# The first mixer's VectorE order: the decay matrix ahead of the convolution taps in slots 2 to 5

## The chip, the cores and the metric

The program runs on one core of a Trainium2 chip. The metric is the device time of one execution in microseconds, lower is better.

## The reference

Two model blocks one after the other, on 512 rows of width 1024, in float32. The change lies in the first mixer of the first block, a state space mixer with 32 heads in 8 groups and chunks of 128 rows, run in both directions:

```python
def step(state, inp):                       # one chunk of 128 rows
    cum = jnp.cumsum(lac, axis=1)
    decay = jnp.exp(jnp.where(causal, cum[:, :, None] - cum[:, None], -jnp.inf))
    xdt = xc * dtc[..., None]
    cb = jnp.einsum('blgn,bsgn->blsg', cc, bc)
    y = jnp.einsum('blsgr,bsgrp->blgrp', cb[..., None] * decay, xdt)
    y = y + jnp.einsum('blgn,bgrpn->blgrp', cc, state) * jnp.exp(cum)[..., None]
    ...                                     # new state
def ssd_mixer(u, w_in, conv_w, ...):
    z, xbc, dt = jnp.split(u @ w_in, ...)
    xbc = jax.nn.silu(dwconv(xbc, conv_w, conv_b))      # five taps
    y = ssd_scan(forward) + rev(ssd_scan(reversed)) + xh * d_skip
    y = rmsnorm(y * jax.nn.silu(z)) @ w_out             # per group
```

After it come a second mixer (gated linear attention), a convolution and attention block, cross attention and an MLP; the change does not touch them.

## The kernel before

All large products are *streamed*. A unit of weights (128 x 1024 numbers, 0.5 MB) is loaded by SP into `weights_raw`, rounded by ScalarE into `weights_hi` (`split_hi`, line 137), and the rest of the rounding is made by VectorE into `weights_lo` (`split_lo`, line 147), which also frees `weights_raw` for a load. TensorE then makes three matmuls for each tile of weights (`mm3`, lines 79 to 81), 24 for a unit, into one of three PSUM banks named `stream` (SB = 3). Tile t uses bank t % 3, and `stream_products` waits for `bank_free` of the tile three before it:

```python
        if t >= SB:
            pe.wait_ge(c.bank_free[t % SB], t // SB)
```

The mixer (`ssd_stage`, line 315) runs in rounds i = 0 to 9 of eight slots k = 0 to 7. In round i, g = i - 1 is the group whose chunks are computed, f = i - 2 the group whose output is normed and multiplied out. Slots 0 and 1 stream the gate z, slots 2, 3, 5 and 6 the four convolution inputs (`CONV`: two tiles of `ssd_x`, then two of `ssd_bc`) of group i, slots 4 and 7 (`SSD_OUT`, from round 2 on) an output unit: four tiles of six matmuls each, every one into its own bank. Rounds 2 to 7 are full; round 1 has nothing in slots 4 and 7; round 8 has no convolution inputs.

Each engine has its own program of the slots, written out by hand, and executes it in order; the loop `for i, k in slots` in each part sets that order. In slot k:

- TensorE streams the slot's unit; then in slots 2 to 4 it makes the state contributions (line 752), in slots 2 to 5 `y_intra(g, k - 2)` (line 734), which multiplies `ssd_m` of block k - 2, and in slots 1 to 4 `decay_sums(g, k - 1)` (lines 708 to 711), the sums from which the decay of block k - 1 is computed.
- ScalarE starts the convolution of the tile of the slot before (centre tap and bias, line 856), rounds the weights of the unit two ahead, and in slots 2 to 5 takes the exponential of the decay sums (`ssd_work`, line 919; semaphore `s_decay`).
- POOL makes in slots 2 to 5 the backward part of block k - 2 (line 681) and in slots 1 to 4 the four step tensors `ssd_la_steps` for the decay sums (line 693), which wait for the decay sums before.
- VectorE adds the other four taps to the convolution of the tile of the slot before (line 983; the last of them frees the bank), closes the output tiles of the slot before (`close`, line 952: adds bank to `h` and frees it), makes the weight rest of the unit two ahead, closes the first output tile of this slot, and then comes to the three operations of the decay matrix for block t = k - 2 (lines 1057, 1061, 1066): `ssd_cb` times dt, plus the backward part, times the decay. The third waits for `s_decay` of its block. After them come the state operations (lines 1074 to 1082) and, in slot 2, the norm of group f (lines 1088, 1091).

Of the kernel before, what the change touches and what calls it, by code (L numbers as in the profile page):

```python
# [15 lines left out]
ALU = mybir.AluOpType  # L16
AX = mybir.AxisListType

P = 128
# [10 lines left out]
HPG = SH // SG  # L30
# [53 lines left out]
def spread(ap, n):  # L84

    return ap.rearrange("p (a o) -> p a o", o=1).broadcast_to([ap.shape[0], ap.shape[1], n])


def again(ap, n):

    return ap.rearrange("p (o a) -> p o a", o=1).broadcast_to([ap.shape[0], n, ap.shape[1]])
# [223 lines left out]
def ssd_stage(nc, c, A, plan, gain):  # L315
# [8 lines left out]
    with ExitStack() as ctx:  # L324
# [4 lines left out]
        dtc = sb("dt_cols", [P, NT, 64])  # L329
# [249 lines left out]
        decay, t1, t2 = (work[:, j, :] for j in range(3))  # L579
        xw = mb("xw", [P, 2, 3, GW])  # L580
        bt = mb("b_tok", [P, T])
        cbm = mb("cb", [P, 2, T])
        rhs = mb("la_steps", [P, 4, HPG, P], F32R)
        mm = mb("m", [P, 2, HPG, P])
# [18 lines left out]
        G = range(SG)  # L603
        CONV = {2: 0, 3: 1, 5: 2, 6: 3}

        def conv_tile(g, j):
            return (2 * g, 2 * g + 1, 2 * SG + g, 3 * SG + g)[j]
# [11 lines left out]
        def head(cols, d, t, g):  # L619
            return cols[:, t, 32 * d + HPG * g:32 * d + HPG * (g + 1)]  # L620
# [4 lines left out]
        def before(i, k):  # L625
            return (i, k - 1) if k else (i - 1, NU - 1)

        def tile_of(i, k):
            return c.tiles_before[plan[i, k]]
# [310 lines left out]
        def _(dve):  # L940
# [30 lines left out]

            for i, k in slots:
                g, f = i - 1, i - 2
                pi, pk = before(i, k)
                if (pi, pk) in plan and pk in CONV:
                    cj = CONV[pk]
                    t, ct = tile_of(pi, pk), conv_tile(pi, cj)
# [48 lines left out]
                if k == 1 and g in G:  # L1026
# [13 lines left out]
                    for d, t0, nt in ((0, 0, 2), (0, 2, 1), (1, 1, 1), (1, 2, 2)):  # L1040
# [5 lines left out]
                                src[:, u * GW:(u + 1) * GW].rearrange("p (h m) -> p h m", h=HPG),  # L1046
                                spread(w[:, u, :], HD), ALU.mult)
                        ins.then_inc(s_xw, 1)
                if 2 <= k <= 5 and g in G:
                    t = k - 2  # L1050
                    m = 3 * (4 * g + t)
                    v = t1.rearrange("p (h l) -> p h l", h=HPG)
                    if t == 0:
                        dve.wait_ge(s_cbm, 2 * g + 2)
                    if 4 * g + t:
                        dve.wait_ge(s_m, m)
                    dve.tensor_tensor(v, again(cbm[:, 0, t * P:(t + 1) * P], HPG),  # L1057
                                      spread(head(dtc, 0, t, g), P), ALU.mult).then_inc(s_m, 1)
                    dve.wait_ge(s_m, m + 1)
                    dve.wait_ge(s_t2, 4 * g + t + 1)  # L1060
                    dve.tensor_tensor(t1, t1, t2, ALU.add).then_inc(s_m, 1)  # L1061
                    dve.wait_ge(s_m, m + 2)
                    dve.wait_ge(s_decay, 4 * g + t + 1)
                    if 4 * g + t >= 2:
                        dve.wait_ge(s_y, 4 * g + t - 1)
                    dve.tensor_tensor(mm[:, t % 2, :, :].rearrange("p h l -> p (h l)"), t1, decay, ALU.mult)\  # L1066
                       .then_inc(s_m, 1)
                if 3 <= k <= 5 and g in G:
                    j = k - 3
                    dve.wait_ge(s_con, 3 * g + j + 1)  # L1070
# [2008 lines left out]
```

## Time and profile before

| | us |
|---|---|
| median of three timed runs | 1860.97 (1857.37 to 1861.91) |
| the profiled execution | 1857.3, span 1855.6 |
| TensorE busy | 1735.0 (94%) |
| VectorE busy | 1189.9 (64%) |
| ScalarE busy | 769.0 (41%) |
| POOL busy | 408.1 (22%) |

Times are counted from the span's start. The first mixer's rounds 1 to 8 lie between some 62 and 580 us. A matmul row shows when the matmul began and its modelled duration; consecutive ones overlap, so the distance of their starts is their price. In square brackets stands how long the engine sat idle before a row, and whom it waited for.

### The profile page before, as it was taken

The page shows a single profiled execution, that of the slowest core. Times are in us where ns is not written, and L with a number is a line of the kernel's source. Part 1 is how long each engine was busy: PE and PEld are TensorE (multiplying, and loading weights), DVE is VectorE, ACT ScalarE, POOL GpSimd, SP SyncE. Part 2 cuts the span into 40 slices and gives each one's busy share as a digit, 9 for nine tenths or more (in the row PEclk, how much of TensorE's full clock was granted, in tenths as well). Part 3 has the DMA queues.
Part 4 walks back from the last instruction along what each step waited for, and adds up shares of the span by engine and source line. Part 5 has one row for each costly group of instructions (what it writes and reads, how often), then busy time and mean ns, then how long its engine had stood idle before and what let it go on. Part 6 is the DMA issues. An engine that isn't in the chain of part 4 may idle for free.

```text
span 1855.6 us, 21247 instructions
## 1 busy us (share of the span) xinstructions
PE 1735.0 (94%) x8104; PEld 1404.2 (76%) x8104; DVE 1189.9 (64%) x1587; ACT 769.0 (41%) x1143; POOL 408.1 (22%) x351
## 2 busy tenths in 40 slices
PE   6989999999987999999999889999999999999997
PEld 4767777787765777878777677888778778888886
DVE  6868878877966747575757676777665553434343
ACT  5333444343343435444445344446454442324232
POOL 0444644653563100000002501222120110000001
PEclk9989999999988999999999899999999999999999
DMA  3312222222210322222212223222323233333331
GB/s 102 91 35 68 67 70 57 60 66 69 57 49 25 86 54 65 80 79 69 76 54 87 63 74 80 62 59 80 103 82 103 88 91 91 103 91 102 92 101 69
DMA packets 253772, 139.18 MB, mean 75 GB/s; under 512 B 26013, under 2 KB 248134, under 8 KB 253670
## 3 DMA queue, kind: packets, MB, share of 16 engines
q1 hardware_dynamic: 253670, 137.82, 26.1%
q8 instruction: 65, 1.06, 0.2%
q14 instruction: 37, 0.30, 0.1%
HBM read 135.70 MB, written 2.10 MB: 74 GB/s over the span
## 4 chain that ended last, share of the span: by engine, by line
PE 58%; DVE 22%; ACT 9%; issue 7%; POOL 4%; DMA 1%; ACTq 0%; DVEq 0%; SPq 0%; POOLq 0%
PE stream L79 16%; PE stream L81 16%; PE stream L80 16%; DVE weights_lo L147 3%; ACT weights_hi L137 2%; DVE ssd_x L983 2%; DVE ssd_work L1061 1%; DVE ssd_bc L983 1%; DVE ssd_work L1057 1%; DVE ssd_y L1088 1%; PE q L1978 1%; PE q L2002 1%; POOL ssd_y L653 1%; PE q L79 1%; PE q L81 1%
## 5 line engine op out<-in xcount | busy, mean ns | idle before, releaser
L79 PE MATMUL stream<-u_lo,weights_hi 128*128 128x512 f32 (+2 forms) x1312 | 525.3, 400 | 17.0 <-DVE h L952 5.1
L81 PE MATMUL stream<-u_hi,weights_hi 128*128 128x512 f32 (+2 forms) x1312 | 514.7, 392 | 0.0
L80 PE MATMUL stream<-u_hi,weights_lo 128*128 128x512 f32 (+2 forms) x1312 | 514.6, 392 | 0.0
L147 DVE TENSOR_TENSOR weights_lo<-weights_raw,weights_hi 128x1024 fp32r<-128x1024 f32 (+4 forms) x269 | 336.3, 1252 | 270.2 <-ACT weights_hi L137 269.9
L137 ACT ACTIVATE weights_hi<-weights_raw 128x1024 fp32r<-128x1024 f32 (+4 forms) x269 | 268.5, 1000 | 444.9 <-PE stream L81 430.4
L79 PEld LDWEIGHTS stream<-u_lo,weights_hi 128*128 128x128 f32 (+2 forms) x1312 | 247.7, 189 | 81.0 <-issue 12.4
L81 PEld LDWEIGHTS stream<-u_hi,weights_hi 128*128 128x128 f32 (+2 forms) x1312 | 247.3, 188 | 54.2 <-issue 0.4
L80 PEld LDWEIGHTS stream<-u_hi,weights_lo 128*128 128x128 f32 (+2 forms) x1312 | 247.4, 189 | 53.9 <-issue 2.9
L217 POOL COPY h_sum_of_squares<-h_squares 128x512 f32<-128x512 f32 x5 | 3.2, 648 | 796.9 <-ACT h_squares L205 796.9
L79 PE MATMUL stream<-mlp_a_lo,weights_hi 128*128 128x512 f32 x256 | 100.2, 391 | 0.0
L81 PE MATMUL stream<-mlp_a_hi,weights_hi 128*128 128x512 f32 x256 | 99.7, 389 | 0.0
L80 PE MATMUL stream<-mlp_a_hi,weights_lo 128*128 128x512 f32 x256 | 99.6, 389 | 0.0
L653 POOL TENSOR_TENSOR ssd_y<-ssd_y,ssd_state_parts 128x384 f32<-128x384 f32 x32 | 33.0, 1032 | 184.3 <-DVE ssd_state_parts L969 182.0
L2853 DVE SCALAR_TENSOR_TENSOR mlp_relu<-stream,h_squares 128x512 f32<-128x512 f32 x32 | 22.1, 691 | 70.2 <-PE stream L81 70.1
L1947 POOL TENSOR_TENSOR mix_conv<-mix_conv,att_tap_products 128x512 f32<-128x512 f32 x30 | 40.2, 1341 | 121.6 <-ACT att_tap_products L2061 119.6
L983 DVE SCALAR_TENSOR_TENSOR ssd_bc<-stream,params,ssd_bc 128x510 f32<-128x510 f32 (+1 forms) x64 | 48.0, 749 | 28.6 <-ACT ssd_bc L856 26.9
L220 POOL TENSOR_TENSOR h_sum_of_squares<-h_sum_of_squares,h_squares 128x512 f32<-128x512 f32 x34 | 48.6, 1428 | 71.3 <-ACT h_squares L205 69.7
L79 PE MATMUL stream<-ssd_y_lo,weights_hi 128*128 128x512 f32 x128 | 53.2, 416 | 8.5 <-DVE ssd_y_lo L1091 5.2
L734 PE MATMUL q<-ssd_m,ssd_x_pair 128*128 128x128 f32 x256 | 36.8, 288 | 22.8 <-DVE ssd_m L1066 22.8
L2130 DVE SCALAR_TENSOR_TENSOR q<-mix_z,params,q 128x512 f32<-128x512 f32 x76 | 57.1, 751 | 1.7
L734 PEld LDWEIGHTS q<-ssd_m,ssd_x_pair 128*128 128x128 f32 x256 | 33.0, 196 | 31.0 <-DVE ssd_m L1066 30.1
L693 POOL TENSOR_TENSOR ssd_la_steps<-mask_ge,ssd_la_hi_cols 128x512 fp32r<-128x512 f32 x32 | 39.3, 1229 | 75.1 <-DVE ssd_la_lo_cols L1009 41.5
(484 smaller groups left out, 3155.9 us busy)
## 6 DMA issues: line engine op xcount, KB each, us to landing
weights_raw<-in_w_mlp_dram SPq DMA_DIRECT2D x64, 512.0 KB, 4.0
weights_raw<-in_ssd_w_in_dram SPq DMA_DIRECT2D x48, 512.0 KB, 3.9
weights_raw<-in_gla_w_in_dram SPq DMA_DIRECT2D x40, 512.0 KB, 3.8
weights_raw<-in_w_in_dram SPq DMA_DIRECT2D x29, 512.0 KB, 3.8
weights_raw<-in_ssd_w_out_dram SPq DMA_DIRECT2D x16, 512.0 KB, 3.6
weights_raw<-in_gla_w_out_dram SPq DMA_DIRECT2D x13, 512.0 KB, 3.4
weights_raw<-in_w_out_dram SPq DMA_DIRECT2D x8, 512.0 KB, 3.9
weights_raw<-in_w_xkv_dram SPq DMA_DIRECT2D x8, 512.0 KB, 3.8
```

The costliest lines, as they stand in the source:

```text
L79: pe.matmul(out, lh, rl, start=first, stop=False, skip_group_check=skip)
L80: pe.matmul(out, ll, rh, start=False, stop=False, skip_group_check=skip)
L81: return pe.matmul(out, lh, rh, start=False, stop=last, skip_group_check=skip)
L137: act.activation(w_view(c, n)[0], raw_view(c, n), ACT.Copy).then_inc(c.w_rounded, 1)
L147: dve.tensor_tensor(lo, raw_view(c, n), hi.bitcast(F32), ALU.subtract).then_inc(c.w_split, 1)
L220: pool.tensor_tensor(acc[:, :], acc[:, :], c.sq[:, n % 2, :], ALU.add).then_inc(c.square_added, 1)
L653: pool.tensor_tensor(y[:, p, a], y[:, p, a], parts[:, d * (T - P):(d + 1) * (T - P)], ALU.add).then_inc(s_fin, 1)
L693: pool.tensor_tensor(rhs[:, j, :, :], again(mask[:, :], HPG), spread(head(part, d, t, g), P), ALU.mult).then_inc(s_rhs, 1)
L734: last = pe.matmul(q[p][:, t * P:(t + 1) * P], xp[:, t, p, a], mm[:, t % 2, 2 * p + h, :], start=h == 0, stop=h == 1, skip_group_check=True)
L983: ins = dve.scalar_tensor_tensor(out=dst[:, a:b], in0=src[:, a + o:b + o], scalar=tap(tp, ct), in1=dst[:, a:b], op0=ALU.mult, op1=ALU.add)
L1947: pool.tensor_tensor(acc[:, LAST, :], acc[:, LAST, :], prod[:, e % 2, :], ALU.add)\
L2130: dve.scalar_tensor_tensor(out=dst, in0=src, scalar=par[:, w:w + 1], in1=q[4][:, :], op0=ALU.mult, op1=ALU.add).then_inc(s_tap, 1)
```

## The change

On VectorE, in slots 2 to 5, the block with the three operations moves from behind the taps, closings and weight rest of the slot to the slot's beginning. Its waits move with it unchanged; no other engine's program changes. By line numbers of the changed kernel the three are lines 982, 986 and 991, and the taps line 1002.

```diff
             for i, k in slots:
                 g, f = i - 1, i - 2
+                if 2 <= k <= 5 and g in G:
+                    t = k - 2
+                    m = 3 * (4 * g + t)
+                    ...
+                    dve.tensor_tensor(v, again(cbm[:, 0, t * P:(t + 1) * P], HPG),
+                                      spread(head(dtc, 0, t, g), P), ALU.mult).then_inc(s_m, 1)
+                    dve.wait_ge(s_m, m + 1)
+                    dve.wait_ge(s_t2, 4 * g + t + 1)
+                    dve.tensor_tensor(t1, t1, t2, ALU.add).then_inc(s_m, 1)
+                    dve.wait_ge(s_m, m + 2)
+                    dve.wait_ge(s_decay, 4 * g + t + 1)
+                    if 4 * g + t >= 2:
+                        dve.wait_ge(s_y, 4 * g + t - 1)
+                    dve.tensor_tensor(mm[:, t % 2, :, :].rearrange("p h l -> p (h l)"), t1, decay, ALU.mult)\
+                       .then_inc(s_m, 1)
                 pi, pk = before(i, k)
                 if (pi, pk) in plan and pk in CONV:
                     ...
                         ins.then_inc(s_xw, 1)
-                if 2 <= k <= 5 and g in G:
-                    ...
                 if 3 <= k <= 5 and g in G:
```

VectorE's program in a full round, from the rest of the output's rounding (`ssd_y_lo`, end of slot 2) through slot 3 into slot 4, before:

```order
L1091 TENSOR_TENSOR ssd_y_lo<-ssd_y,ssd_y_hi 128x1024
L983 SCALAR_TENSOR_TENSOR ssd_x<-stream,params,ssd_x 128x510
L983 SCALAR_TENSOR_TENSOR ssd_x<-stream,params,ssd_x 128x511 x2
L983 SCALAR_TENSOR_TENSOR ssd_x<-stream,params,ssd_x 128x510
L147 TENSOR_TENSOR weights_lo<-weights_raw,weights_hi 128x1024
L1057 TENSOR_TENSOR ssd_work<-ssd_cb,ssd_dt_cols 128x512
L1061 TENSOR_TENSOR ssd_work<-ssd_work 128x512
L1066 TENSOR_TENSOR ssd_m<-ssd_work 128x512
L1074 COPY ssd_state<-q 128x512
L983 SCALAR_TENSOR_TENSOR ssd_x<-stream,params,ssd_x 128x510
```

The same place in the changed program:

```order
L1091 TENSOR_TENSOR ssd_y_lo<-ssd_y,ssd_y_hi 128x1024
L982 TENSOR_TENSOR ssd_work<-ssd_cb,ssd_dt_cols 128x512
L986 TENSOR_TENSOR ssd_work<-ssd_work 128x512
L991 TENSOR_TENSOR ssd_m<-ssd_work 128x512
L1002 SCALAR_TENSOR_TENSOR ssd_x<-stream,params,ssd_x 128x510
L1002 SCALAR_TENSOR_TENSOR ssd_x<-stream,params,ssd_x 128x511 x2
L1002 SCALAR_TENSOR_TENSOR ssd_x<-stream,params,ssd_x 128x510
L147 TENSOR_TENSOR weights_lo<-weights_raw,weights_hi 128x1024
L1074 COPY ssd_state<-q 128x512
L982 TENSOR_TENSOR ssd_work<-ssd_cb,ssd_dt_cols 128x512
L986 TENSOR_TENSOR ssd_work<-ssd_work 128x512
```

The three operations of slot 3 have passed four taps and a weight rest; those of slot 4 stand ahead of the second tile's taps. VectorE's program from slot 4's weight rest (the closing with `h` behind it is that of slot 4's first output tile) into slot 5, before:

```order
L147 TENSOR_TENSOR weights_lo<-weights_raw,weights_hi 128x1024
L952 TENSOR_TENSOR h<-h,stream 128x512
L1057 TENSOR_TENSOR ssd_work<-ssd_cb,ssd_dt_cols 128x512
L1061 TENSOR_TENSOR ssd_work<-ssd_work 128x512
L1066 TENSOR_TENSOR ssd_m<-ssd_work 128x512
L1079 TENSOR_TENSOR ssd_state<-ssd_state,ssd_total_cols 128x256 x2
L1082 TENSOR_TENSOR ssd_state<-ssd_state,q 128x512
L952 TENSOR_TENSOR h<-h,stream 128x512 x3
```

The same place in the changed program:

```order
L147 TENSOR_TENSOR weights_lo<-weights_raw,weights_hi 128x1024
L952 TENSOR_TENSOR h<-h,stream 128x512
L1079 TENSOR_TENSOR ssd_state<-ssd_state,ssd_total_cols 128x256 x2
L1082 TENSOR_TENSOR ssd_state<-ssd_state,q 128x512
L982 TENSOR_TENSOR ssd_work<-ssd_cb,ssd_dt_cols 128x512
L986 TENSOR_TENSOR ssd_work<-ssd_work 128x512
L991 TENSOR_TENSOR ssd_m<-ssd_work 128x512
L952 TENSOR_TENSOR h<-h,stream 128x512 x3
```

The three closings of slot 5 now stand behind slot 5's decay matrix, where before they stood ahead of it.

## Rows read from the trace of the kernel before

**Rows 1.** The page: the span, and TensorE's busy time, share and instructions.

```profile
span 1855.6 us, 21247 instructions
PE 1735.0 (94%) x8104; PEld 1404.2 (76%) x8104; DVE 1189.9 (64%) x1587; ACT 769.0 (41%) x1143; POOL 408.1 (22%) x351
```

**Rows 2.** Waits of TensorE, 70 to 600 us: total, times, longest.

```profile
PE q L734 <- DVE ssd_m L1066: 22.8, 18, 4.7
PE stream L79 <- DVE h L952: 5.5, 7, 0.8
```

**Rows 3.** TensorE's timeline, rounds 3 and 4: start, duration, operation, count, idle before.

```profile
223.59 1.16 PE L734 MATMUL q<-ssd_m,ssd_x_pair 128*128 128x128 f32 x8 [1.47 <-DVE ssd_m L1066]
...
286.86 1.02 PE L752 MATMUL q<-ssd_xw,ssd_b_tok 128*128 128x256 f32 x4
289.34 1.16 PE L734 MATMUL q<-ssd_m,ssd_x_pair 128*128 128x128 f32 x8 [1.45 <-DVE ssd_m L1066]
...
291.26 0.39 PE L79 MATMUL stream<-ssd_y_lo,weights_hi 128*128 128x512 f32 x1
...
294.01 0.39 PE L79 MATMUL stream<-ssd_y_lo,weights_hi 128*128 128x512 f32 x1
...
295.37 0.42 PE L79 MATMUL stream<-ssd_y_lo,weights_hi 128*128 128x512 f32 x1
...
296.77 1.02 PE L752 MATMUL q<-ssd_xw,ssd_b_tok 128*128 128x256 f32 x4
298.31 1.16 PE L734 MATMUL q<-ssd_m,ssd_x_pair 128*128 128x128 f32 x8 [0.51 <-DVE ssd_m L1066]
...
300.00 0.39 PE L711 MATMUL q<-ssd_la_steps,mask_lt 128*128 128x512 f32 x1
301.23 0.47 PE L79 MATMUL stream<-u_lo,weights_hi 128*128 128x512 f32 x1 [0.84 <-DVE h L952]
```

**Rows 4.** VectorE's timeline, round 4, slots 2 to 5.

```profile
272.30 1.21 DVE L147 TENSOR_TENSOR weights_lo<-weights_raw,weights_hi 128x1024 fp32r<-128x1024 f32 x1
...
281.02 1.22 DVE L1091 TENSOR_TENSOR ssd_y_lo<-ssd_y,ssd_y_hi 128x1024 fp32r<-128x1024 f32 x1 [1.12 <-ACT ssd_y_hi L924]
282.17 3.10 DVE L983 SCALAR_TENSOR_TENSOR ssd_x<-stream,params,ssd_x 128x510 f32<-128x510 f32 x4
285.18 2.05 DVE L147 TENSOR_TENSOR weights_lo<-weights_raw,weights_hi 128x1024 fp32r<-128x1024 f32 x1
287.15 0.68 DVE L1057 TENSOR_TENSOR ssd_work<-ssd_cb,ssd_dt_cols 128x512 f32<-128x512 f32 x1
...
289.80 3.09 DVE L983 SCALAR_TENSOR_TENSOR ssd_x<-stream,params,ssd_x 128x510 f32<-128x510 f32 x4
292.81 1.82 DVE L147 TENSOR_TENSOR weights_lo<-weights_raw,weights_hi 128x1024 fp32r<-128x1024 f32 x1
...
300.40 1.88 DVE L952 TENSOR_TENSOR h<-h,stream 128x512 f32<-128x512 f32 x3
```

**Rows 5.** ScalarE's decay of slot 5, and POOL's steps of slot 3, round 4.

```profile
300.43 0.60 ACT L919 ACTIVATE ssd_work<-q 128x512 f32<-128x512 f32 x1 [2.34 <-PE q L711]
...
281.64 1.50 POOL L693 TENSOR_TENSOR ssd_la_steps<-mask_ge,ssd_la_hi_cols 128x512 fp32r<-128x512 f32 x1 [0.85 <-PE q L711]
```

**Rows 6.** VectorE's timeline, round 1, slot 3: operations beside POOL's steps.

```profile
87.83 1.52 DVE L1057 TENSOR_TENSOR ssd_work<-ssd_cb,ssd_dt_cols 128x512 f32<-128x512 f32 x1
89.39 1.41 DVE L1061 TENSOR_TENSOR ssd_work<-ssd_work 128x512 f32<-128x512 f32 x1
```

**Rows 7.** Long waits of TensorE, and two stretches: busy times, then granted clock (PEclk).

```profile
100.00 2.07 PE L734 MATMUL q<-ssd_m,ssd_x_pair 128*128 128x128 f32 x8 [4.75 <-DVE ssd_m L1066]
...
564.71 1.38 PE L734 MATMUL q<-ssd_m,ssd_x_pair 128*128 128x128 f32 x8 [2.72 <-DVE ssd_m L1066]
...
1000.36 0.50 PE L79 MATMUL stream<-gla_k_lo,weights_hi 128*128 128x512 f32 x1 [2.47 <-DVE gla_k_lo L1451]
...
100.00:105.00 5.00, 5.00 (x16) 4.37 (x17) 4.90 (x7) 0.60 (x1) 0.84 (x1) 0.53 0.07 16
590.00:594.00 4.00, 4.00 (x12) 3.21 (x13) 0.88 (x2) 0.41 (x1) 0.00 (x0) 0.65 0.53 148
```

More of the change, by code:

```diff
@@ L973, in _ @@
                 g, f = i - 1, i - 2
+                if 2 <= k <= 5 and g in G:
+                    t = k - 2
+                    m = 3 * (4 * g + t)
+                    v = t1.rearrange("p (h l) -> p h l", h=HPG)
+                    if t == 0:
+                        dve.wait_ge(s_cbm, 2 * g + 2)
+                    if 4 * g + t:
+                        dve.wait_ge(s_m, m)
+                    dve.tensor_tensor(v, again(cbm[:, 0, t * P:(t + 1) * P], HPG),
[9 more added lines that the diff above has]
+                       .then_inc(s_m, 1)
                 pi, pk = before(i, k)
@@ L1048, in _ @@
                         ins.then_inc(s_xw, 1)
-                if 2 <= k <= 5 and g in G:
[L1050 to L1067, printed above, removed]
                 if 3 <= k <= 5 and g in G:
```

## The prediction

> **What bounds the kernel now.** I read the profile's page first: TensorE is busy for 94% of the span [rows 1], so the question is where the first mixer makes TensorE wait, and whether the new order makes those waits shorter or longer. The view of the waits on TensorE between 70 and 600 us comes next [rows 2]: the longest entry is the one that the moved operations can remove, 22.8 us over 18 waits of the line 734 products for `ssd_m` (I call the three operations for block t together M(t)). Then the timeline of TensorE over slots 3 to 5 of round 4 [rows 3]. The same wait stands 65.75 us earlier, at 223.59, so rounds 2 to 7 repeat one pattern and six rounds can be priced by one. A round has three waits that concern us: 1.45 us ahead of y_intra(1), 0.51 ahead of y_intra(2), and 0.84 ahead of slot 5's stream, which waits for a closing `h` + bank (line 952).
>
> What to see in the timelines of VectorE [rows 4] is that it has no idle time from 282.17 to 302: taps (3.1 us), rest of the weights, M(1), copy, taps again, rest, and so on. Its order decides who gets his release late.
>
> **What the change moves.** It adds and removes no instruction. On VectorE, M goes ahead of up to three things: in slot 3 ahead of the taps of the first `x` tile and a weight rest; in slot 4 ahead of the taps of the second `x` tile, a rest and the first closing; in slot 5 ahead of three closings and a rest. The code shows what the passed-over work releases. The stream has three PSUM banks. Slot 4 streams an output unit of four tiles of 6 matmuls. Its tile 2 (the third) takes the bank that the taps in slot 4 free, its tile 3 the bank of the first closing, and slot 5's stream the bank of the second closing. Before, the taps end at 289.80 + 3.09 = 292.9, 1.1 us ahead of tile 2 at 294.01, and the first closing (a closing is 0.63 us, from 1.88 for three) ends near 295.2, 0.15 ahead of tile 3 at 295.37 [rows 3, 4]. That cover is thin, and M(2) is put in front of it.
>
> *Slot 3.* M(1) no longer waits for taps and rest, so y_intra(1) follows the line 752 products after 0.86 us, which is their distance where nothing waits. It starts at 287.7 instead of 289.34; its eight products also take 0.1 less. TensorE is 1.7 us ahead and starts slot 4's stream at 289.55 instead of 291.26. Tile 2 could start 2.75 us later (294.01 - 291.26), at 292.3.
>
> *Slot 4.* When do the taps end now? Price of M: 2.0 us where POOL is still (from 287.15, with `ssd_m` seen by TensorE at 289.34). Where POOL makes the decay steps at the same time, each of the three operations takes 1.4 to 1.5, so 4.3 in all [rows 6]. POOL makes these steps from 281.64 on [rows 5], four of 1.0 to 1.5 each, and again as soon as the decay sums of slot 3 are out, near 289.7. M(1) and M(2) now both fall into these stretches; before, they fell behind them. I take 3.9 for each, near the upper end. In slot 2 the rest of the weights changes from a quiet place (1.21) to a crowded one (2.05) and makes everything after it 0 to 0.8 later; I take 0.7. The chain on VectorE is then: 282.2 + 0.7 = 282.9; M(1) 286.8; taps 289.8; rest 1.6 (between 1.21 and 2.05) 291.4; copy 0.6, 292.0; M(2) 295.9; taps 299.0. So tile 2 waits from 292.3 to 299.0, 6.7 us, and starts 5.0 us later than before.
>
> Tile 3 then needs rest and closing (1.14 + 0.67) against a tile of 1.36, 0.45 more. But behind a wait of this length the clock is low: in 100 to 105 us, after the wait of 4.75, the granted clock is 0.53 of full, in 590 to 594 us it is 0.65 [rows 7]. That is 1.2 GHz for 4.7 and for 2.8 us. Half of it is lost: 1.4 to 2.35 us. This hides the 0.45; I take 1.6 for both.
>
> *y_intra(2)* does not wait now, -0.7, and its products are 0.1 shorter: -0.8.
>
> *Slot 5.* M(3) must wait for its decay, which ScalarE can compute only when TensorE has made the last decay sum, just ahead of the stream; the second closing stands behind it. From the start of the last sum (line 711): 0.43 to ScalarE [rows 5], 0.60 its work, 0.05, 0.61 for the product, 0.67 for the closing, 0.15 to TensorE: 2.5 us. Before, it was 301.23 - 300.00 = 1.23. So +1.3. The rest for slot 7 and closings two and three are late too, but they are wanted 5 us and more later, so at nothing.
>
> One steady round: 5.0 + 1.6 - 0.8 + 1.3 = +7.1 us; six rounds, +42.6.
>
> *Where it gains.* Round 1 has no output unit in slot 4, and TensorE waits 4.75 us for M(2) behind 3.09 of taps: -3.0, and up to -2.2 more if the clock stays up (the eight products took 2.07 instead of 1.16). Round 8 has no taps; M(3) waits 2.72 us behind three closings; the decay allows 1.3 of it [rows 7]. Bounds -4.3 and -8; I take -5.5. The first slots of a round, ScalarE, POOL and SP keep their order; a weight load begins once the rest is split off, up to 4 us later now, and is wanted two slots (some 16 us) on. Nothing.
>
> **Sum.** 42.6 - 5.5 = +37. The profiled execution took 1857.3 us (span 1855.6 and 1.7 around it), 3.7 below the median of the three timed runs, 1860.97, and inside their spread. 1857.3 + 37 = 1894.4; I say 1895.
>
> **The page that bears on M's price.** The trace has an `ssd_work` sum at 0.7 alone and 1.41 beside POOL's steps [rows 6]. The Trainium skill, "SBUF — State Buffer", in its section on which operations grab the shared pair, says that a `tensor_tensor` with both inputs in SBUF contends with GpSimd's reads; the page's model is a lock that one instruction holds while the other blocks. By that rule each of M's operations stands behind one of POOL's wherever the two meet, which is the 4.3 end; a reader who goes by it alone would put 0.4 more on each M and come to about 1900. The trace agrees with the rule in rounds 1 and 4.
>
> **Rivals.**
> *Little contention.* POOL's steps and M miss each other: M costs 2.0 to 3 each and the rests 1.2. The taps end near 296.5 instead of 299.0. The other terms stay: 7.1 - 2.5 = 4.6, six times is 28, less 5.5: +22, 1879.5. For it: before, M and the steps mostly miss each other. Against: POOL starts on the very event that M waits for.
> *The floor, and no slowdown.* VectorE keeps up so well that M(2)'s last product is bound only by its decay. The last sum of slot 3 would start at 289.3; + 0.43 + 0.60 + 0.05 + 0.61 + 3.09 of taps = 294.1. Tile 2 is then 0.1 late, tile 3 0.45 more, no slow clock (a wait of 1.8), - 0.8, + 1.3: +1.05 a round, +6.3. Rounds 1 and 8 give back 4.3 to 8.8: 1855 to 1859, about 1857, not slower. It decides when the chain of slots 2 to 4 on VectorE is shorter than 294.1 - 282.2 = 11.9 us; its work without any contention is just that (2.0 + 3.0 + 1.2 + 0.6 + 2.0 + 3.1), so it needs all contention gone. Against it: rows 6.
> *The clock.* (a) It stays up behind the wait in slot 4: 1.15 less a round, 1888. (b) It falls behind slot 5's wait as well, which is about 2.3 us long: +1.6 a round, 1905. A wait of 2.47 at 1000.36 was followed by a first matmul of 0.50 [rows 7], one of 4.75 by slow ones; so (b) is not likely, and (a) less.
> *It does what it says?* The order shows it; no chance of its own. That the gain is all there is (22.8 us of waits gone, 1834) would need the taps' bank not to be waited for; the code has that wait.
>
> **Chances.** Forecast 60%, with 1887 to 1905 as its own range. Little contention 19%, clock stays up 6%, clock falls twice 9%, floor 5%, a gain after all 1%. The range for 8 in 10: below it the floor and the quiet end of little contention (about 10%), above it the worst of two clock falls: 1874 to 1908. What a measurement can tell from no change is 0.3%, 5.6 us around 1861. Slower: all but the floor and the gain, 94%; the floor is mostly "same": 0.04; faster 0.02.
>
> **What would show it.** Right: in rounds 2 to 7 TensorE's waits for `ssd_m` in slots 3 and 4 are gone; in the middle of slot 4's stream stands a wait of about 6.7 us for the `ssd_x` taps (12 matmuls after its start), matmuls at half clock behind it; ahead of slot 5's stream the wait for `h` is some 2.1 instead of 0.84; a round is near 72.9 instead of 65.75. In round 1 the 4.75 has become 1 to 2. Wrong: the wait in slot 4 under 3 us (contention), or none (then the bank is free in another way than I read it), or rounds no longer.

## The result, and the profile after

| | before | changed |
|---|---|---|
| median of four runs, us | 1861.44 (1857.37 to 1863.25) | 1903.90 (1900.94 to 1905.15) |
| profiled execution's span, us | 1855.6 | 1902.8 |
| TensorE busy | 1735.0 | 1753.7 (92%) |

The changed kernel is slower by 2.3%: the ratio is 1.0229, 95% interval 1.0208 to 1.025. The forecast was 1895, with 1874 to 1908 as the range.

The waits of TensorE from 70 to 600 us, changed kernel (total, times, longest), against those of before [rows 2]:

```profile
PE stream L79 <- DVE ssd_x L1002: 34.9, 6, 5.8
PE stream L79 <- DVE h L952: 13.2, 7, 2.2
...
PE q L734 <- DVE ssd_m L991: 3.8, 3, 1.8
```

The wait for `ssd_m` is nearly gone, 22.8 us over the mixer before. In its place stands one that was not there, six times 5.8 us for the taps of `ssd_x`, and the wait for `h` has grown. TensorE in round 4, slots 3 to 5, changed kernel (compare [rows 3]; the round begins 13.1 us later than in the kernel before, at 275.35 instead of 262.27, by the first transpose of `ssd_x`):

```profile
300.81 1.05 PE L734 MATMUL q<-ssd_m,ssd_x_pair 128*128 128x128 f32 x8
...
302.64 0.39 PE L79 MATMUL stream<-ssd_y_lo,weights_hi 128*128 128x512 f32 x1
...
305.15 0.39 PE L81 MATMUL stream<-ssd_y_hi,weights_hi 128*128 128x512 f32 x1
311.35 0.79 PE L79 MATMUL stream<-ssd_y_lo,weights_hi 128*128 128x512 f32 x1 [5.81 <-DVE ssd_x L1002]
...
315.87 1.02 PE L752 MATMUL q<-ssd_xw,ssd_b_tok 128*128 128x256 f32 x4
316.73 1.05 PE L734 MATMUL q<-ssd_m,ssd_x_pair 128*128 128x128 f32 x8
...
318.32 0.40 PE L711 MATMUL q<-ssd_la_steps,mask_lt 128*128 128x512 f32 x1
320.88 0.47 PE L79 MATMUL stream<-u_lo,weights_hi 128*128 128x512 f32 x1 [2.16 <-DVE h L952]
```

Twelve matmuls of the output unit run, then TensorE stops for tile 2. Neither y_intra row (300.81, 316.73) has a wait. From tile 2 to the line 752 row are 4.52 us; before it was 296.77 - 294.01 = 2.76. From the last decay sum to the next stream: 2.56, before 1.23. VectorE in the same stretch (compare [rows 4]):

```profile
295.38 1.53 DVE L982 TENSOR_TENSOR ssd_work<-ssd_cb,ssd_dt_cols 128x512 f32<-128x512 f32 x1
296.94 1.41 DVE L986 TENSOR_TENSOR ssd_work<-ssd_work 128x512 f32<-128x512 f32 x1
298.39 1.41 DVE L991 TENSOR_TENSOR ssd_m<-ssd_work 128x512 f32<-128x512 f32 x1
299.72 3.09 DVE L1002 SCALAR_TENSOR_TENSOR ssd_x<-stream,params,ssd_x 128x510 f32<-128x510 f32 x4
302.73 1.22 DVE L147 TENSOR_TENSOR weights_lo<-weights_raw,weights_hi 128x1024 fp32r<-128x1024 f32 x1
...
304.46 0.93 DVE L982 TENSOR_TENSOR ssd_work<-ssd_cb,ssd_dt_cols 128x512 f32<-128x512 f32 x1
305.43 1.41 DVE L986 TENSOR_TENSOR ssd_work<-ssd_work 128x512 f32<-128x512 f32 x1
306.87 1.41 DVE L991 TENSOR_TENSOR ssd_m<-ssd_work 128x512 f32<-128x512 f32 x1
308.21 3.09 DVE L1002 SCALAR_TENSOR_TENSOR ssd_x<-stream,params,ssd_x 128x510 f32<-128x510 f32 x4
...
319.44 0.69 DVE L991 TENSOR_TENSOR ssd_m<-ssd_work 128x512 f32<-128x512 f32 x1 [3.69 <-ACT ssd_work L919]
320.05 1.88 DVE L952 TENSOR_TENSOR h<-h,stream 128x512 f32<-128x512 f32 x3
```

VectorE has no idle time until the taps end at 311.30, 0.05 ahead of tile 2. M(1) takes 4.34, M(2) 3.75 (from 304.46 to 308.21). In slot 5 it sits idle 3.69 us until ScalarE has the decay, with the closings that TensorE needs behind it. The steps on POOL that M runs beside:

```profile
302.88 1.96 POOL L693 TENSOR_TENSOR ssd_la_steps<-mask_ge,ssd_la_hi_cols 128x512 fp32r<-128x512 f32 x1 [1.19 <-PE q L711]
304.81 1.48 POOL L693 TENSOR_TENSOR ssd_la_steps<-mask_ge,ssd_la_lo_cols 128x512 fp32r<-128x512 f32 x1
```

Granted clock (the third number from the end) behind the wait in slot 4, behind that in slot 5 of round 4, and behind that in slot 5 of round 3:

```profile
311.40:315.00 3.60, 3.60 (x9) 2.83 (x10) 3.56 (x6) 0.00 (x0) 0.00 (x0) 0.50 0.35 89
321.00:326.00 5.00, 5.00 (x16) 3.93 (x17) 3.42 (x6) 0.00 (x0) 0.00 (x0) 0.66 0.33 88
247.00:252.00 5.00, 3.39 (x15) 2.87 (x16) 4.79 (x8) 0.09 (x1) 0.00 (x0) 1.00 0.02 6
```

The clock is at its lower level, 1.2 GHz, behind the wait in slot 4, and behind slot 5's wait as well in round 4, but not in round 3. It falls there in rounds 2, 4 and 6.

**By stretches.** Taken from one round's first transpose of `ssd_x` to the next one's (the last stretch from the first matmul of the last output units to the end):

| profiled run, us | round 1 | rounds 2 to 7 | one of them | round 8 | behind the mixer |
|---|---|---|---|---|---|
| before | 62.4 | 394.7 | 65.8 | 64.7 | 1265.7 |
| changed | 60.7 | 440.3 | 73.4 | 63.7 | 1270.2 |

Rounds 2 to 7 bring +45.6, the first and the last -2.7, together +42.9. The stretch behind the mixer, whose program is the same, is 1265.8 to 1272.1 us in the other kernels below, so 4.5 us of the difference of the spans (47) lie where nothing was changed; the profiled execution of before (1857.3) is 4 below its median. The medians differ by 42.5.

### The profile page after: what moved, and what is told of

It reads as the page before. It is cut to its first block, busy times and chain, and to the rows that moved or that the text cites. A ratio compares the mean times of both kernels' runs of the same rounds, so it can differ in the third digit from the quotient of the medians.

```text
span 1902.8 us, 21247 instructions
## 1 busy us (share of the span) xinstructions
PE 1753.7 (92%) x8104; PEld 1418.9 (75%) x8104; DVE 1188.2 (62%) x1587; ACT 769.4 (40%) x1143; POOL 415.0 (22%) x351
## 3 DMA queue, kind: packets, MB, share of 16 engines
q8 instruction: 65, 1.06, 0.2%
## 4 chain that ended last, share of the span: by engine, by line
PE 62%; DVE 18%; ACT 9%; issue 6%; POOL 4%; DMA 1%; ACTq 0%; DVEq 0%; SPq 0%; POOLq 0%
PE stream L79 17%; PE stream L80 17%; PE stream L81 17%; DVE weights_lo L147 3%; ACT weights_hi L137 2%; DVE ssd_x L1002 2%; DVE ssd_bc L1002 1%; DVE ssd_m L991 1%; DVE ssd_y L1088 1%; PE q L1978 1%; PE q L2002 1%; DVE ssd_work L986 1%; POOL ssd_y L653 1%; PE q L79 1%; PE q L81 1%
## 5 line engine op out<-in xcount | busy, mean ns | idle before, releaser
L79 PE MATMUL stream<-ssd_y_lo,weights_hi 128*128 128x512 f32 x128 | 58.8, 459 | 43.5 <-DVE ssd_x L1002 34.9
L79 PEld LDWEIGHTS stream<-ssd_y_lo,weights_hi 128*128 128x128 f32 x128 | 27.8, 217 | 56.8 <-DVE ssd_x L1002 37.4
L693 POOL TENSOR_TENSOR ssd_la_steps<-mask_ge,ssd_la_hi_cols 128x512 fp32r<-128x512 f32 x32 | 43.3, 1353 | 76.2 <-DVE ssd_la_lo_cols L1028 41.5
L80 PE MATMUL stream<-ssd_y_hi,weights_lo 128*128 128x512 f32 x128 | 56.0, 437 | 0.0
```

The lines of the kernel that those rows point to most:

```text
L79: pe.matmul(out, lh, rl, start=first, stop=False, skip_group_check=skip)
L80: pe.matmul(out, ll, rh, start=False, stop=False, skip_group_check=skip)
L693: pool.tensor_tensor(rhs[:, j, :, :], again(mask[:, :], HPG), spread(head(part, d, t, g), P), ALU.mult).then_inc(s_rhs, 1)
```

## The experiments

In all, the three operations stand in a function, `decay_matrix`, with their text unchanged, and VectorE's program decides where it is called. "Rounds 2 to 7" and the round times are those of the profiled execution of each kernel; the first number of each result is the median of its executions.

**Slot 4 alone.**

```diff
+                if k in (4,) and g in G:
+                    decay_matrix(g, k)
                 pi, pk = before(i, k)
...
+                if 2 <= k <= 5 and g in G and k not in (4,):
+                    decay_matrix(g, k)
                 if 3 <= k <= 5 and g in G:
```

The first call stands ahead of the taps, the second, for the other slots, where the operations stood in the kernel before.

> The three operations stand ahead in slot 4 alone. Theory A (a bank is released late: what VectorE does ahead of the taps of slot 4 delays tile 2 of the output unit): the 1.45 wait for ssd_m in slot 3 stays, tile 2 waits about 2.5 us for the ssd_x taps in rounds 2 to 7, tile 3 0.45 more, y_intra(2) does not wait, round 1 gains 3: +10 us, 1871. Rival B (what costs is that M runs beside POOL's steps in slots 2 and 3, not what stands behind it): no more than 3 us off the time before, 1861.

Measured: 1869.56 against 1860.70, ratio 1.0054 (1.0037 to 1.0071). TensorE's waits, 70 to 600 us:

```profile
PE q L734 <- DVE ssd_m L990: 14.6, 12, 2.1
PE stream L79 <- DVE ssd_x L1006: 12.0, 6, 2.0
```

Six waits of 2.0 for the taps (2.5 expected); rounds 2 to 7 take 408.8, +14.2, round 1 58.4, -4.0. Theory A holds, rival B falls: slots 2 and 3 were not touched. The clock has a part in it too: rounds 2 and 3, where it stayed up, cost 1.5 and 1.6 more than before, and rounds 4 to 7, where it fell behind the wait of 2.0, 2.2 to 4.1.

**Slot 5 alone** (the same with `(5,)`).

> Ahead in slot 5 alone. Theory A: the wait for the second closing ahead of slot 5's stream goes from 0.84 to 2.1 in rounds 2 to 7, +1.3 a round, the last round gains 1.3: +6.5 us, 1868; if the clock falls behind that wait in every second round, as it did in the changed kernel, 5 more. Rival B: same time, 1861.

Measured: 1890.06, ratio 1.0149 (1.0128 to 1.0169). A miss for theory A's size. VectorE, and then TensorE, round 4:

```profile
305.19 0.69 DVE L990 TENSOR_TENSOR ssd_m<-ssd_work 128x512 f32<-128x512 f32 x1
...
308.03 0.68 DVE L981 TENSOR_TENSOR ssd_work<-ssd_cb,ssd_dt_cols 128x512 f32<-128x512 f32 x1
...
310.08 1.88 DVE L952 TENSOR_TENSOR h<-h,stream 128x512 f32<-128x512 f32 x3
```

```profile
310.91 0.47 PE L79 MATMUL stream<-u_lo,weights_hi 128*128 128x512 f32 x1 [2.90 <-DVE h L952]
```

Here the decay is not what M(3) waits for: VectorE itself is late from slot 4, and all three operations, 2.05 us, stand ahead of the closing. The wait is 2.90, not 2.16. The round in which the clock stayed up (round 4) took 67.79, the 2.0 more that the longer wait gives; the other five, behind each of which the granted clock fell, 69.3 to 70.6. Together +22.8 in rounds 2 to 7. So slot 5's price has two parts: the wait, and a clock fall that it may or may not bring. The second varies from execution to execution: the profiled one took 1882.22 at a mean granted clock of 0.975, the other three 1890.05 to 1890.91 at 0.967 to 0.969, so the median cost is 29.4, more than this trace shows.

**Slots 2 and 3 alone.**

> Ahead in slots 2 and 3 alone. Theory A: y_intra(1) does not wait, slot 4's stream starts 1.7 us earlier, but taps and copy of slot 4 end near 295.7 on the clock of the kernel before, so tile 2 waits 3.3, tile 3 0.45, and M(2) is about 1.7 later than before: +2 us a round, +12, 1873. Rival C (slots 2 and 3 bring a pure gain, the loss is all from slots 4 and 5): six times -1.6, 1851.

Measured: 1864.09, ratio 1.0019 (1.001 to 1.0028), rounds 2 to 7 +2.0 (+12 expected).

The gain at y_intra(1) and the new wait for the taps (six times 2.1, 3.3 expected) nearly cancel. VectorE ends slot 4's taps 1.6 us later in the round than before: POOL adds 2.3 to M(1), and the weight rest behind it is 0.8 cheaper. Theory A had the sign and six times the size in these rounds: the taps were 1.2 us earlier than it said, and M(2), which it had 1.7 late, ended only 0.2 late, since in this kernel each of its operations took 0.7. Rival C falls. The clock fell behind the wait of 2.1 in three of the six rounds.

**Slot 5 put back** (slots 2, 3 and 4 ahead).

> The changed kernel with slot 5 put back. Theory A: the wait for the taps in slot 4 stays 5.8, the wait for the closing is gone from slot 5 except what VectorE's backlog leaves (0 to 0.8): -1.3 to -2.2 a round, and no second clock fall: rounds 2 to 7 take 424 to 430 us instead of 440, 1888 to 1893. Rival G (TensorE then waits for M(3) at the end of slot 5 instead): 1900.

Measured: 1883.12, ratio 1.0119 (1.0104 to 1.0134).

```profile
PE stream L79 <- DVE ssd_x L1006: 34.8, 6, 5.8
```

The wait for the taps is 5.8 again; no wait of 0.3 or more stands ahead of slot 5's stream. Rounds 2 to 7 take 421.4, 18.9 less than changed: 3.1 a round, of which 2.33 is the distance that goes (2.56 - 0.23), the other 0.8 the clock, which no longer falls a second time in any round. That is a little below the 424 to 430 that were expected, since slot 5's wait is gone wholly. Rival G falls.

**Slot 4's taps put back** (slots 2, 3 and 5 ahead; in slot 4 taps and first closing first).

```diff
+                if k == 4 and (i, k) in SSD_OUT:
+                    close(i, k, 0)
+                if k in (4,) and g in G:
+                    decay_matrix(g, k)
                 if unit_in(i, k) is not None:
                     split_lo(c, dve, unit_in(i, k) + 2)
...
```

> The changed kernel, but in slot 4 the taps and the first closing go ahead of the three operations. Theory A: the wait for the taps is that of the kernel with slots 2 and 3 alone, 2.1 instead of 5.8, little or no slow clock behind it, y_intra(2) may wait up to 1; slot 5's wait stays 2.2 to 2.9 with its clock falls: rounds 2 to 7 take 410 to 420, 1873 to 1883.

Measured: 1881.13, ratio 1.0108 (1.0093 to 1.0123).

```profile
PE stream L79 <- DVE h L952: 14.7, 6, 3.1
PE stream L79 <- DVE ssd_x L1006: 12.3, 6, 2.1
```

The wait for the taps is 2.1, and rounds 2 to 7 take 415.9, as expected: the place of the operations in slot 4 is worth 24.4 of the 45.6. One part was not expected: the clock fell behind the wait of 2.1 in four of the six rounds, where little or none of that was looked for.

**The wait filled with matmuls.**

```diff
+        if filler and j == 2:
+            filler()
         if t >= SB:
             pe.wait_ge(c.bank_free[t % SB], t // SB)
...
+                        def filler():
+                            pe.wait_ge(s_decay, 4 * g + 3)
+                            for _ in range(24):
+                                pe.matmul(q[4][:, :], c.gt_r[:, :], c.uh[:, 0, :],
+                                          start=True, stop=True)
```

The filler first waits until ScalarE has read the decay sums of M(2) from `q[4]`; its results are used by nobody.

> The changed kernel with 24 extra matmuls (5.4 us at full clock, into a bank that is free) ahead of tile 2 of slot 4's unit in rounds 2 to 7, where TensorE waits 5.8 us for the taps. Theory A (the clock falls because of this wait and costs 1.8 a round in slot 4, and its after-effect lets it fall again in slot 5 of every second round): tile 2 starts when it did, the matmuls behind it run at full clock, a round is 1.8 to 2.5 shorter: -11 to -15, near 1890. Rival D (the time behind the wait is VectorE's, not the clock's): 1904 or more.

Measured: 1894.45, ratio 1.0182 (1.0167 to 1.0197): 9.5 us less than changed (11 to 15 expected), with 144 matmuls more. Round 4 on TensorE, and the clock behind the wait:

```profile
302.86 5.60 PE L779 MATMUL q<-u_hi,mask_gt 128*128 128x512 f32 x24
308.84 0.50 PE L79 MATMUL stream<-ssd_y_lo,weights_hi 128*128 128x512 f32 x1 [0.38 <-DVE ssd_x L1015]
...
312.06 1.02 PE L754 MATMUL q<-ssd_xw,ssd_b_tok 128*128 128x256 f32 x4
...
317.06 0.47 PE L79 MATMUL stream<-u_lo,weights_hi 128*128 128x512 f32 x1 [2.16 <-DVE h L961]
```

```profile
308.00:313.00 5.00, 4.55 (x20) 3.15 (x19) 4.90 (x8) 0.68 (x1) 0.00 (x0) 1.00 0.38 99
```

Tile 2 begins 36.0 us into the round, as in the changed kernel. From there to line 752's row (754 here) it is 3.22 instead of 4.52: the slow clock is gone, and the 0.45 for tile 3's closing, which it had hidden, comes out; net 1.3 in this round, and some 0.6 more in every second one, as is shown further down. The first half of theory A holds: the time behind the wait in slot 4 is the clock's. The second half, that the fall in slot 5 is an after-effect of slot 4's, doesn't: without a fall in slot 4, three of six rounds (3, 5 and 7) still had one behind slot 5's wait. A wait of 2.16 is enough in some rounds.

**POOL's steps shortened**, in the changed kernel and, as a control, in the kernel before.

```diff
-                        pool.tensor_tensor(rhs[:, j, :, :], again(mask[:, :], HPG),
-                                           spread(head(part, d, t, g), P), ALU.mult).then_inc(s_rhs, 1)
+                        n = P if g == 0 else 8
+                        pool.tensor_tensor(rhs[:, j, :, 0:n], again(mask[:, 0:n], HPG),
+                                           spread(head(part, d, t, g), n), ALU.mult).then_inc(s_rhs, 1)
```

> The changed kernel; from the second group on POOL computes only 8 of 128 columns of each step tensor, so the decays are not the reference's. M no longer runs beside POOL's steps. Theory A (order plus contention): M(1) and M(2) cost 2.0 each instead of 4.3 and 3.7, the wait for the taps in slot 4 falls from 5.8 to about 1.8, no clock fall, the wait for the closing in slot 5 stays 2.2: rounds 2 to 7 cost +1.3 each instead of +7.6, about 1866. Rival E (order alone, the contention is a side show): the wait stays above 4, 1895 or more.

> The kernel before with the same 8 of 128 columns, as the control. In it M already runs beside a quiet POOL mostly; the weight rest of slots 3 and 4 gets 0.8 cheaper: the wait of 1.45 in slot 3 falls to about 0.6, rounds 2 to 7 gain about 1 each, 1853.

From the second group on both kernels leave out 120 of 128 columns of each step tensor, so what they return is not the reference's; they serve for the times alone.

Measured: 1865.09 (ratio to the kernel before 1.0024, 1.0013 to 1.0035) and 1826.84 (0.9821, 0.9798 to 0.9844). TensorE's wait, and VectorE in slots 3 and 4 of round 4, changed kernel with short steps:

```profile
PE stream L79 <- DVE ssd_x L1007: 10.7, 6, 1.8
```

```profile
281.00 0.68 DVE L982 TENSOR_TENSOR ssd_work<-ssd_cb,ssd_dt_cols 128x512 f32<-128x512 f32 x1
281.72 0.69 DVE L986 TENSOR_TENSOR ssd_work<-ssd_work 128x512 f32<-128x512 f32 x1
...
290.85 0.73 DVE L991 TENSOR_TENSOR ssd_m<-ssd_work 128x512 f32<-128x512 f32 x1 [1.32 <-ACT ssd_work L920]
```

The operations take 0.7 instead of 1.4, and the wait falls from 5.8 to 1.8, to where the decay of M(2) is what comes last: the floor of the prediction, 1.8 as it was worked out there. Contention with POOL is thus 4.0 of the 5.8; theory A holds there, rival E falls. (Shorter steps also make the decay sums possible sooner, but in rounds 2 to 7 these wait for POOL in neither kernel.) Theory A expected no clock fall and got one in every round, so a round costs 2.1 more than before (67.9 against 65.8), not 1.3; that the time is still near the 1866 expected is luck, for rounds 1 and 8 took 3.3 and 8.2 less than before. And the control missed by 26 us: the old order loses 4.1 a round to POOL too (65.8 against 61.7, with no wait of 0.3 or more left in rounds 2 to 7; 1 was expected), and round 8 another 9.6. Against this control the new order costs 38 us. So contention makes the wait long; it does not make the order bad. Without POOL the order still costs 6.2 a round (67.9 - 61.7): waits of 1.8 and 2.2, and a clock fall in each round.

**A better order.** Nothing stands ahead of taps; the operations pass the weight rest alone; slot 4's first closing goes ahead of them, its second right behind them.

```diff
+                if k == 4 and (i, k) in SSD_OUT:
+                    close(i, k, 0)
+                if k in (3, 4) and g in G:
+                    decay_matrix(g, k)
+                if k == 4 and (i, k) in SSD_OUT:
+                    close(i, k, 1)
                 if unit_in(i, k) is not None:
                     split_lo(c, dve, unit_in(i, k) + 2)
...
```

> Nothing stands ahead of taps: in slots 3 and 4 the three operations go ahead of the weight rest only, behind the taps; in slot 4 the first closing goes ahead of them and the second closing right behind them, instead of in slot 5. Slots 2 and 5 as before. Theory A: the wait for ssd_m in slot 3 falls from 1.45 to about 0.3, in slot 4 stays near 0.5, the 0.84 for the closing goes: -2.2 us a round, -13, 1848. Rival B: the moved weight rests and the operations beside POOL eat it: 1861 within 4.

Measured: 1851.26, ratio 0.9946 (0.9933 to 0.9958).

```profile
284.71 1.16 PE L734 MATMUL q<-ssd_m,ssd_x_pair 128*128 128x128 f32 x8 [0.31 <-DVE ssd_m L990]
...
290.30 0.50 PE L79 MATMUL stream<-ssd_y_lo,weights_hi 128*128 128x512 f32 x1 [0.79 <-DVE ssd_x L1004]
```

Rounds 2 to 7 take 382.8, -11.9: y_intra(1) waits 0.31 instead of 1.45, y_intra(2) and slot 5's stream less than 0.3, and 0.8 appears for the taps. Two steps further from it:

```diff
+                full = 2 <= i <= 7
...
+                if k == 4 and full:
+                    split_lo(c, dve, unit_in(i, k) + 1)
                 if unit_in(i, k) is not None:
-                    split_lo(c, dve, unit_in(i, k) + 2)
+                    if not (k == 3 and full):
+                        split_lo(c, dve, unit_in(i, k) + 2)
```

> From the kernel of the reordered slots 3 and 4 (1851): in rounds 2 to 7 slot 3's weight rest moves behind slot 4's second closing; rounds 1 and 8 have the operations ahead in slot 4 alone. Theory A: the 0.8 wait for the taps goes, rounds 2 to 7 another -0.8 each, round 1 -4, round 8 -2: 1840. Rival F (the later weight rest makes the load for slot 7's unit late, and ScalarE, which waits for it, delays the decay of slot 5): 1851 or more.

Measured: 1857.95, ratio 0.9983 (0.9971 to 0.9994). The 0.8 for the taps is gone and round 1 takes 58.4, but rounds 2 to 7 take 398.8, 16.0 more than the kernel it starts from. Rival F is what happened; ScalarE in slot 5 of round 4:

```profile
300.11 1.06 ACT L137 ACTIVATE weights_hi<-weights_raw 128x1024 fp32r<-128x1024 f32 x1 [10.71 <-DMA weights_raw<-in_ssd_w_out_dram]
301.08 0.58 ACT L919 ACTIVATE ssd_work<-q 128x512 f32<-128x512 f32 x1
```

The late rest starts the load late, ScalarE waits for the load, and the decay of slot 5 stands behind it in ScalarE's order: y_intra(3) waits 2.1 to 3.7. With the rests where they were, and the operations ahead in slot 4 alone in rounds 1 and 8:

> The kernel of the reordered slots 3 and 4 in rounds 2 to 7, weight rests where they were; rounds 1 and 8 have the operations ahead in slot 4 alone. Theory A: rounds 2 to 7 take 383 as in that kernel, round 1 58.4 instead of 62.1, round 8 61 to 62 instead of 65.9: 1842 to 1844. Rival: the savings at the ends are given back in the next stage: 1850.

Measured: 1843.52, ratio 0.9903 (0.9887 to 0.992), the fastest of those that compute what the reference does. Rounds 2 to 7 take 382.9; rounds 1 and 8 61.4 and 62.7. Of the 3.7 that round 1 was to bring only 0.8 came. Its program in round 1 is that of the kernel just above, which took 58.4; the clock was low in part of 68 to 73 us and of 99 to 104 us here (0.66 in each, so 1.7 us lost in each), and full in both there, which covers the difference of 2.9. Of the 17.4 us between the medians the profiled executions show 14.7 in rounds 1 to 8.

## Why the prediction was right

**The mechanism was the one named.** In rounds 2 to 7 the waits for `ssd_m` are gone, the wait for the `ssd_x` taps stands 12 matmuls into slot 4's stream, the clock is low behind it, and slot 5's wait is 2.16, where "some 2.1" was said. The tests with one part put back show slot 4 as the larger part (24.4 of the 45.6 in rounds 2 to 7) and slot 5 as the smaller (18.9). Moved alone, the parts are otherwise: 3.4 us for slots 2 and 3, 8.9 for slot 4, 29.4 for slot 5 by the medians, 41.7 together against 42.5. That this sum comes out is no sign that the parts are independent: moving slots 2 and 3 makes slot 4's wait longer (2.0 to 5.8), a late TensorE makes slot 5's shorter (2.90 to 2.16), and the traces of rounds 2 to 7 add to 39.0 only (2.0 + 14.2 + 22.8), that of slot 5 being the fastest of its four executions.

**Term by term, for a steady round.** The round's start being put at zero, tile 2 begins at 36.0 (311.35 - 275.35), before at 31.7 (294.01 - 262.27): +4.3, forecast +5.0. Two M's at 4.34 and 3.75 were near the forecast 3.9 (8.1 in all against 7.8). The weight rest of slot 3 was 1.13, not 1.6: it began 0.15 ahead of POOL's step at 302.88, and that one got long, 1.96. The delay from slot 2 was 0.1, not 0.7: the rest there did take 2.06 instead of 1.21, but M(0), now ahead of it, met less of POOL and gave back 0.7, a term that the forecast had left out. From tile 2 to line 752: +1.76, forecast +1.6. y_intra(2): -0.8, as forecast. Slot 5: +1.33, forecast +1.3. Their sum is +6.6 for round 4. Measured is 7.6 in the mean of six rounds, forecast 7.1. What is missing is clock, and the rounds alternate. Granted clock from tile 2 on in round 3, then in round 4:

```profile
238.60:245.60 7.00, 7.00 (x26) 5.81 (x27) 4.29 (x7) 1.06 (x1) 0.00 (x0) 0.67 0.28 75
311.40:318.40 7.00, 7.00 (x28) 5.75 (x28) 4.28 (x7) 1.06 (x1) 0.00 (x0) 0.75 0.27 75
```

In round 3 it is 0.67 over 7 us, in round 4 0.75: 2.3 against 1.75 us lost. From tile 2 to slot 5's stream rounds 3, 5 and 7 take 10.05 to 10.08, rounds 2, 4 and 6 9.48 to 9.54. So rounds 3, 5 and 7 cost 6.6 + 0.5 = 7.1 and have no second fall, and rounds 2, 4 and 6 cost 6.6 and 1.7 for the fall behind slot 5's wait (0.66 over the 5 us from 321), 8.3 by this sum and 8.2 measured. The mean measured is 7.6.

**The step that was mis-sized: rival (b) of the clock.** It was given 9% as an affair of all rounds, on one wait of 2.47 that was followed by a quick matmul. It came in rounds 2, 4 and 6, where it costs 1.7, so +0.8 in the mean. With slot 5 alone and a wait of 2.9 it came in five of six. The fall behind slot 4's wait was mis-sized by less: +0.3 in the mean, from the longer stretch in every second round. Against these two stands the early tile 2, -0.7.

**The base.** The forecast added its 37 to the profiled execution, 1857.3, and not to the median. The median of before came out as 1861.44, so 4.1 of the 8.9 us between 1895 and 1903.9 are this choice of base, the largest single part; rounds 2 to 7 are 3.0 (45.6 against 42.6) and the ends 2.8. These come to 9.9, which is 1.0 too much: 0.6 of it is the rounding up to 1895, and 0.4 the difference between 42.9 and 42.5.

**The ends.** -5.5 was taken, -2.7 came. (Of the upper bounds that the prediction gives for this gain, 8 and 8.8, its rows carry the first: 5.2 + 2.7.) Round 1 gained 1.7 instead of at least 3. TensorE, round 1, changed kernel:

```profile
96.53 1.16 PE L734 MATMUL q<-ssd_m,ssd_x_pair 128*128 128x128 f32 x8 [1.06 <-DVE ssd_m L991]
99.42 0.50 PE L708 MATMUL q<-ssd_la_steps,mask_gt 128*128 128x512 f32 x1 [1.73 <-POOL ssd_la_steps L693]
...
100.03 0.63 PE L710 MATMUL q<-ssd_la_steps,mask_lt 128*128 128x512 f32 x1
```

The 4.75 became 1.06, but the decay sums behind it now wait 1.73 for POOL's steps, a wait that the old one had covered. I had asked for M(2) what was late next, and not for the sums. That is one half of it. The other is the clock, which fell behind this wait and once more near 69 us (0.66 over 68 to 73 us, where the kernel before has 1.00): with slot 4 alone, where it did neither, the sums waited 1.74 as well and round 1 gained 4.0. Round 8 gained 1.0 in the same way: the wait of 2.72 became 1.47, and the products of line 765 behind it now wait 1.79 for `ssd_state`.

**The rule on the shared pair.** The rule of the Trainium skill, "SBUF — State Buffer", in its section on who interferes with whom, that a `tensor_tensor` of two SBUF inputs contends with GpSimd's reads, was borne out by the test that takes most of POOL's work away: 1.41 became 0.69, and the wait in slot 4 fell from 5.8 to 1.8. As a strict lock it would be too hard: side by side the two engines' operations follow each other every 1.45 us (305.43 to 306.87 on VectorE, 304.81 to 306.25 on POOL), while alone they take 0.7 and 1.0 from start to start, 1.7 together. The 1900 that the rule alone gave is nearer to the 1903.9 than my 1895, but by chance: it corrects the term (M at 4.3) that was right enough, and not those that were off.

**What stays open.** Why a wait of 2.0 to 2.2 makes the clock fall in some rounds and not in others, and why the low stretch behind slot 4's wait is longer in every second round. The runs here do not tell.

## What to carry to other kernels

Before an operation is moved ahead of others on an in-order engine, list what the passed-over operations release and how much slack each release has in the timeline: here 22.8 us of waits were in sight, while the taps' bank had 1.1 us of slack and a closing 0.15, with no row among the waits to show it. An operation that itself waits for the engine it serves (M for the decay of the last sum) should stand behind all that this engine wants meanwhile: with slot 5 put back, 3.1 us a round went. And a moved operation meets other neighbours: it took twice as long beside the other engine's work. Last, add a forecast difference to the median of the timed executions, not to the one that happened to be profiled.

## What was not expected of the hardware

In rounds 2 to 7, waits of 5.8 us amid dense matmuls brought the granted clock down in six of six rounds (changed kernel), of 2.90 in five of six (slot 5 alone), of 2.16 in three of six (changed kernel, and again with the filler). Waits of 2.0 to 2.1 in slot 4 did it in four of six with slot 4 alone, in three of six with slots 2 and 3 alone, and in four of six with slot 4's taps put back. The waits of 1.45 of the kernel before never did. With short POOL steps, a wait of 1.8 and one of 2.2 some 6 us later brought one fall in every round, in one of the six behind the first of the two. Shortening POOL's steps alone made the kernel before 34 us faster (1861.1 to 1826.8), although POOL is busy for only 22% of its span.
